# Softmax heads' first values by probabilities in three rounded products

## The reference

```python
def chunk_rel_attention(q, k, v, qn_g, kn_g, rel_bias):
    ...
    sc = jnp.where(valid[None, None, :, None, :], sc, NEG)
    p = jax.nn.softmax(sc, axis=-1)
    o = jnp.einsum('bhnqk,bnkhd->bhnqd', p, vb)
```

## Time and profile before

| | value |
|---|---|
| median of three executions | 1798.87 us (1797.88 to 1799.27) |
| the profiled execution: its own time | 1798.44 us |
| its span, first to last instruction | 1796.5 us |
| PE busy | 1786.8 us, 99% |
| DVE busy | 1246.1 us, 69% |
| ACT busy | 1052.9 us, 59% |
| POOL busy | 217.0 us, 12% |
| PE's granted clock, mean of the span | 0.999 of full speed |

### The profile page before, as it was taken

The page is one execution under the profiler, slowest core; times in us unless marked ns, Lnnn a source line. Parts: engine busy times, 40 slices in busy tenths (PEclk is TensorE's granted clock), DMA queues, the critical chain, the costliest instruction groups (busy, mean ns, idle before and its releaser), DMA issues.

```text
span 1796.5 us, 27448 instructions
## 1 busy us (share of the span) xinstructions
PE 1786.8 (99%) x10874; PEld 1621.4 (90%) x10874; DVE 1246.1 (69%) x1711; ACT 1052.9 (59%) x1702; POOL 217.0 (12%) x180
## 2 busy tenths in 40 slices
PE   9999999999999999999999999999999999999998
PEld 8999889888899999998889999898888999989987
DVE  6665656665666897687668888766565888767764
ACT  7436546774557765875554345686454445458853
POOL 0000000110011111100001322011000132311210
PEclk9999999999999999999999999999999999999999
DMA  9657555555655555454566655555565665555564
GB/s 367 199 175 223 186 182 190 178 177 192 193 185 173 167 173 169 155 172 164 190 209 201 202 190 177 194 177 175 188 191 197 200 199 186 174 191 182 172 220 140
DMA packets 95903, 340.32 MB, mean 189 GB/s; under 512 B 10800, under 2 KB 11184, under 8 KB 95648
## 3 DMA queue, kind: packets, MB, share of 16 engines
q1 hardware_dynamic: 94400, 334.44, 56.6%
q0 software_dynamic: 944, 3.61, 0.7%
q10 hardware_dynamic: 432, 0.53, 0.1%
HBM read 336.44 MB, written 2.10 MB: 188 GB/s over the span
## 4 chain that ended last, share of the span: by engine, by line
PE 99%; DMA 0%; DVE 0%; ACT 0%; issue 0%; DVEq 0%
PE ACC L848 15%; PE ACC L850 15%; PE ACC L849 15%; PE ACC L856 12%; PE ACC L853 12%; PE ACC L855 6%; PE ACC L854 6%; PE ACC L861 2%; PE ACC L862 2%; PE ACC L863 2%; PE PM L1015 1%; PE PM L993 1%; PE PM L900 1%; PE PM L970 0%; PE PM L1016 0%; PE PM L1063 0%
## 5 line engine op out<-in xcount | busy, mean ns | idle before, releaser
L1680 DVE TENSOR_TENSOR WL<-RAW,WH 128x1024 fp32r<-128x1024 f32 (+2 forms) x631 | 795.4, 1276 | 418.6 <-ACT WH L1239 417.2
L1239 ACT ACTIVATE WH<-RAW 128x1024 fp32r<-128x1024 f32 (+2 forms) x632 | 647.6, 1038 | 371.4 <-PE ACC L850 185.3
L856 PE MATMUL ACC<-XHL,WH 128*128 128x512 f32 x1024 | 391.2, 382 | 0.0
L853 PE MATMUL ACC<-XHL,WH 128*128 128x512 f32 x1024 | 390.3, 381 | 0.0
L848 PE MATMUL ACC<-WH,XHL 128*128 128x512 f32 (+1 forms) x788 | 295.9, 376 | 0.2 <-DVE WL L1680 0.2
L850 PE MATMUL ACC<-WH,XHL 128*128 128x512 f32 (+1 forms) x788 | 291.9, 370 | 0.0
L849 PE MATMUL ACC<-WL,XHL 128*128 128x512 f32 (+1 forms) x788 | 291.9, 370 | 0.0
L855 PE MATMUL ACC<-XHL,WL 128*128 128x256 f32 x1024 | 281.6, 275 | 0.0
L854 PE MATMUL ACC<-XHL,WL 128*128 128x256 f32 x1024 | 279.1, 273 | 0.0
L855 PEld LDWEIGHTS ACC<-XHL,WL 128*128 128x128 f32 x1024 | 193.5, 189 | 27.5
L854 PEld LDWEIGHTS ACC<-XHL,WL 128*128 128x128 f32 x1024 | 193.6, 189 | 25.9
(11 more groups left out here) (414 smaller groups left out, 2451.6 us busy)
## 6 DMA issues: line engine op xcount, KB each, us to landing
RAW<-in_w SPq DMA_DIRECT2D x607, 512.0 KB, 3.3
RAW<-in_wv SPq DMA_DIRECT2D x24, 344.0 KB, 3.2
X<-in_x SPq DMA_DIRECT2D x4, 512.0 KB, 12.1
Y<-in_xT SPq DMA_DIRECT2D x3, 512.0 KB, 10.7
out<-Y SPq DMA_DIRECT2D x6, 256.0 KB, 3.6
S<-in_bias POOLq DMA_DIRECT2D x8, 128.0 KB, 2.3
S<-in_od_gate_w POOLq DMA_DIRECT2D x1, 1024.0 KB, 7.3
S<-in_final_norm POOLq DMA_DIRECT2D x1, 1024.0 KB, 6.3
```

The lines of the kernel that those rows point to most:

```text
L853: e.matmul(acc[0], wh0, pairs, start=f, stop=False, skip_group_check=True)
L856: m = e.matmul(acc[1], wh1, pairs, start=False, stop=l, skip_group_check=True)
L1239: e.activation(hi, src, ACT.Copy).then_inc(s_hi)
L1680: e.tensor_tensor(lo, src, hi.bitcast(F32), ALU.subtract).then_inc(s_lo)
```

## The change

For the 32 heads with values 128 wide, the product of `v[0]` by the probabilities of all 256 tokens, one F32 product so far, becomes three rounded ones: high values by high probabilities, low by high, high by low. The product of `v[1]` stays in F32.

- `pT`, ACT: copies only the last 128 of the 384 columns as they are; the first 256 go rounded into `PH`, in a second instruction. It waits for the `pv` of the head before.
- `pl`, DVE, new: subtracts `PH` from PSUM into `PL`, 256 columns. It stands two slots after `pT`, in `after`; in the first eight heads of layer 3 half a slot after it, so in `before` of the next slot, ahead of the rope job's evacuation. The bank of PSUM is free for others only after it.
- `value_split`, new: three slots ahead of `pT`, ACT copies `v[0]` rounded (128 columns), and POOL subtracts (128 columns).
- `pv`, PE: waits for the low parts of the values and of the probabilities besides.
- The new buffer PVH takes the place of ZC, which is used in layer 1 alone. No bank and no transfer is added.

```diff
+        PH, PL = PVH[:, 0:256], PVH[:, 256:512]
...
                         put(slot + every * r + late, step, first + h + (4 if step[0] == "p" else 0), 1)
+                        if step == "pT":
+                            put(slot + every * r + late - 3, "value_split", first + h + 4)
+                            put(slot + every * r + (0.5 if first == 24 else 2) + late, "pl", first + h + 4)
...
-                read_out[b] = (s_pts, TURN[g])
+                read_out[b] = (s_pl, nth_narrow(g)) if narrow(g) else (s_pts, TURN[g])
...
                 if dv == 128:
-                    e.matmul(o[:, 0:256], v[0], p[:, 0:256], start=True, stop=False, skip_group_check=True)
+                    vh, vl = value_slot(g)
+                    e.wait_ge(s_vl, nth_narrow(g))
+                    e.wait_ge(s_pl, nth_narrow(g))
+                    e.matmul(o[:, 0:256], vh, PH, start=True, stop=False, skip_group_check=True)
+                    e.matmul(o[:, 0:256], vl, PH, start=False, stop=False, skip_group_check=True)
+                    e.matmul(o[:, 0:256], vh, PL, start=False, stop=False, skip_group_check=True)
                     e.matmul(o[:, 128:256], v[1], p[:, 256:384], start=False, stop=True, skip_group_check=True).then_inc(s_pv)
...
             def pT(g, b):
                 e.wait_ge(s_pt, TURN[g])
-                e.activation(pt_slot(g), PM[b][:, 0:384], ACT.Copy).then_inc(s_pts)
+                if not narrow(g):
+                    e.activation(pt_slot(g), PM[b][:, 0:384], ACT.Copy).then_inc(s_pts)
+                    return
+                if g > 4:
+                    e.wait_ge(s_pv, TURN[g] - 1)
+                e.activation(pt_slot(g)[:, 256:384], PM[b][:, 256:384], ACT.Copy).then_inc(s_pts)
+                e.activation(PH, PM[b][:, 0:256], ACT.Copy).then_inc(s_ph)
+
+            def value_split(g, _):
+                v, job = values_at(g)
+                n = nth_narrow(g)
+                e.wait_ge(s_evA, at_A(*job))
+                if n > 2:
+                    e.wait_ge(s_pv, TURN[g] - 2)
+                e.activation(value_slot(g)[0], v[0], ACT.Copy).then_inc(s_vh)
...
+            def probabilities_low(g, _):
+                b = PT_BANK[g]
+                e.wait_ge(s_ph, nth_narrow(g))
+                e.tensor_tensor(PL, PM[b][:, 0:256], PH.bitcast(F32), ALU.subtract).then_inc(s_pl)
...
+            def value_split(g, _):
+                v, _ = values_at(g)
+                vh, vl = value_slot(g)
+                e.wait_ge(s_vh, nth_narrow(g))
+                e.tensor_tensor(vl, v[0], vh.bitcast(F32), ALU.subtract).then_inc(s_vl)
```

More of the change, by code:

```diff
@@ L197, in program @@
         C = sb("C", CW)
-        ZC = sb("ZC", 1024)
+        with ExitStack() as first:
+            ZC = sb("ZC", 1024, F32, first)
+        PVH = sb("PVH", 1024, F32R)
         S5 = sb("S5", 2048)
@@ L278, in half_slot, with value_slot @@
             return [HALF[:, at + x:at + y] for x, y in ((0, 128), (128, 256), (256, 512), (512, 768))]
+        PH, PL = PVH[:, 0:256], PVH[:, 256:512]
+        def value_slot(g):
+            at = 512 + 256 * (g % 2)
+            return PVH[:, at:at + 128], PVH[:, at + 128:at + 256]
         def sc_slot(g):
@@ L416, in program, with values_at, narrow, nth_narrow @@
         TURN = list(accumulate(0 if g >= 4 and first_of_pair(g - 4) else 1 for g in range(44)))
+        def values_at(g):
+            layer, n, h = head_of(g - 4)
+            c = slice(128 * h, 128 * h + 128)
+            return [tok(3 * n + 2 if layer else 5)[:, t, c] for t in range(2)], (layer, f"v{n}" if layer else "va", h // 4)
+        def narrow(g):
+            return g >= 4 and not is_diff(g - 4)
+        def nth_narrow(g):
+            return g - 3 if g < 12 else g - 11
         def masked(a):
@@ L623, in program @@
                     FEW_BANK = got[0]
+        PT_BANK = {item: got for x in plan.values() for step, item, got in x if step == "pT"}
         def around(p):
@@ L657, in program @@
             sem(n) for n in ("s_dg", "s_pa", "s_pe", "s_pk", "s_pc", "s_pm", "s_zero", "s_am", "s_tri", "s_la"))
-        s_neg, s_hh, s_hl = sem("s_neg"), sem("s_hh"), sem("s_hl")
+        s_neg, s_hh, s_hl, s_ph, s_pl, s_vh, s_vl = (
+            sem(n) for n in ("s_neg", "s_hh", "s_hl", "s_ph", "s_pl", "s_vh", "s_vl"))
         s_lx, s_lc, s_ly, s_ld, s_so, s_sd, s_sa, s_or, s_on, s_gd1 = (
@@ L1004, in values_of @@
                     return [tok(2)[:, t, c] for t in range(2)], 256, (2, "v0", h // 4)
-                c = slice(128 * h, 128 * h + 128)
-                return [tok(3 * n + 2 if layer else 5)[:, t, c] for t in range(2)], 128, (layer, f"v{n}" if layer else "va", h // 4)
+                v, job = values_at(g)
+                return v, 128, job
             def pv(g, b):
@@ L1620, in scalar @@
             steps = {"seed": seed, "warm": warm, "xt": xt, "squares": squares, "root": root, "rms_a": rms_a, "gates1": gates1, "selectors": selectors, "decay_cols": decay_cols,
-                     "decay_rows": decay_rows, "cols": columns_step, "rows": rows, "decay": decay, "pT": pT,
+                     "decay_rows": decay_rows, "cols": columns_step, "rows": rows, "decay": decay, "pT": pT, "value_split": value_split,
                      "norm_qk": norm_qk, "qkT": qkT, "halves": halves, "scores": scores, "normal": normal, "silu_z": silu_z, "yT": yT, "mix1": mix1, "pv": pv, "ty": ty, "copied": copied, "silu": silu, "decays1": decays1,
@@ L2162, in vector @@
                      "decay": decay, "mscores": mscores, "norm_qk": norm_qk, "scale_k": scale_k, "scores": scores, "mix1": mix1,
-                     "mix2": mix2, "rsum": rsum, "pv": pv,
+                     "mix2": mix2, "rsum": rsum, "pl": probabilities_low, "pv": pv,
                      "yT": yT, "ty": ty, "taps": taps,
@@ L2320, in gained @@
                     e.tensor_tensor(Y3[:, t, c], X3[:, t, c], S0[:, c], ALU.mult).then_inc(s_gn)
-            steps = {"norm_qk": norm_qk, "scale_k": scale_k, "halves": halves, "scores": scores, "gate_z": gate_z, "cols": columns_step, "tri": tri, "gate_w": gate_w,
+            steps = {"norm_qk": norm_qk, "scale_k": scale_k, "halves": halves, "scores": scores, "value_split": value_split, "gate_z": gate_z, "cols": columns_step, "tri": tri, "gate_w": gate_w,
                      "gate_lru": gate_lru, "gate_c": gate_c, "load_mask": load_mask, "load_gain": load_gain, "gained": gained}
```

## The result

The changed kernel takes 1800.88 us (median of 22 executions, 1799.58 to 1803.43), against 1798.77 us before (median of 22, 1797.82 to 1800.30): 1.0013 times as long, 95% interval 1.0007 to 1.0019. That is 2.1 us slower where 2.3 was forecast: clear of the noise, but within the 0.2% that count as no change. The profiled execution took 1799.58 us, its span 1797.8.

What follows compares the result with a forecast made beforehand. PE, busy 99% of the span, sets the time. A 4.66 us delay in layer 3's first eight heads, less 0.24 given back and 2.1 saved, made 2.3 us slower: 1801.2 us on the median, range 1798.2 to 1804.2.

Steps and rivals of the forecast that it cites:

- PE's own part: Each changed head's pv group on PE falls from 0.65 to 0.57 us, 0.08 less; 2.6 us over 32 heads.
- The loop: ACT and DVE in layer 3's first eight heads: 0.07 plus 0.34, together 0.41 us more each round, on a 13.11 us period.
- Where it comes due: Layer 3's first eight heads: pv waits for the low part, reached at heads 32, 33, 34; PE 4.66 us later.
- None elsewhere: New pv waits on DVE's subtraction, about 3, 4 to 5 us in sum, only between 1545 and 1582 us.
- costed this rounding at nothing: ACT's rounding of `v[0]` falls where ACT waits 6.4 us for DVE; without that cover, 8 x 0.2 us.
- The sum: Whole kernel: 4.66 lost, less 0.24 given back and 2.1 saved by 26 heads, net 2.3 us slower.
- No stall: Rival: the loop gives way or the low part is ready earlier; 2.6 us faster, 3.2 at most; chance 0.13.
- POOL on DVE's port: Rival: POOL's added instruction gets ahead of DVE's waiting split, 0.4 us more a round; net 4.7 us slower; chance 0.18.
- No gain on PE: Rival: three rounded products cost what the F32 one did, stall as forecast; 4.4 us slower; chance 0.06.

Runs made afterwards that it cites:

- The extra subtraction: First eight heads of layer 3 back in F32, plus a DVE subtraction of 256 columns each round, result unused; 1799.12 us, ratio 1.0002 to the kernel before.
- The low part ahead of the split: Changed kernel, but in layer 3's first eight heads `pl` stands before DVE's next weight split; 1796.63 us, ratio 0.9987 to the kernel before.
- the low part early everywhere: Changed kernel, `pl` before the split in layer 3's first eight heads, ahead of the evacuation in all others; 1796.38 us, ratio 0.9989 to the kernel before.
- the low part behind the evacuation: Changed kernel, but in layer 3's first eight heads `pl` stands behind the rope evacuation of its slot; 1807.81 us, ratio 1.0045 to the kernel before.
- the stage alone: Change made only in layer 3's first eight heads, the other 24 keep the F32 product; 1804.74 us, ratio 1.0031 to the kernel before.

## Why the prediction was right, step by step

**PE's own part.** Right: 0.57 us for the group, from the scores' rows. Through layer 0 and layer 2 PE gains 0.61 us each over 8 heads, 0.076 a head, where 0.08 was taken.

**The loop.** Right: 13.50 us forecast and measured. DVE's part was 0.33 (0.34 taken), ACT's copies 0.42 (0.42 worked out, 0.07 in all taken for them). The extra subtraction shows that the added time isn't absorbed. The low part ahead of the split shows that it depends on the place: this the prediction did not see. It treated the loop as one that takes any addition in full.

**Where it comes due.** Right in place and size: 4.66 us forecast at head 34 and 4.66 measured from head 29 on (4.58 from head 28 on, from where the forecast counts), reached at heads 32, 33 and 34, the waits 4.5 us in sum. The savings of heads 28 to 33 are lost in it, and the 0.24 us of the earlier trace rows come back.

**"None elsewhere".** Wrong. Head 42 waits. The prediction costed the low part outside the first eight heads at nothing from head 41's margin, and reasoned that "the 0.4 us don't add up from round to round". From head 36 to head 40 that holds, in the two rounds behind them it does not. These are zT's evacuations of heads 40 and 42 on DVE and the pv of head 42 on PE, before, and then DVE after, at heads 40, 41 and 42:

```profile
1683.58 0.69 DVE L1705 TENSOR_TENSOR S<-S,ROWZ 128x512 f32<-128x512 f32 x1
...
1707.87 0.69 DVE L1705 TENSOR_TENSOR S<-S,ROWZ 128x512 f32<-128x512 f32 x1
...
1710.06 0.59 PE L1015 MATMUL PM<-SC,S 128*128 128x256 f32 x2
```

```profile
1684.86 0.69 DVE L1752 TENSOR_TENSOR S<-S,ROWZ 128x512 f32<-128x512 f32 x1
...
1697.87 0.69 DVE L1752 TENSOR_TENSOR S<-S,ROWZ 128x512 f32<-128x512 f32 x1
...
1710.26 0.69 DVE L1752 TENSOR_TENSOR S<-S,ROWZ 128x512 f32<-128x512 f32 x1
1710.87 0.42 DVE L1979 TENSOR_TENSOR PVH<-PM,PVH 128x256 fp32r<-128x256 f32 x1
```

DVE is 1684.86 - 1683.58 = 1.28 us later than before at head 40, 1697.87 - 1696.03 = 1.84 at head 41, and 1710.26 - 1707.87 = 2.39 at head 42: 0.56 and 0.55 us more in a round. PE is about 1 us later at all three (at head 42 1711.43 less its loss of 0.4, against 1710.06). Set against PE in this way, DVE is about 0.26 us late at each of heads 36 to 40 and no more from head to head, then 0.88 and 1.42. At head 42 the margin was 1.24 us: in the old times the low part would be ready at 1708.48 (where DVE's next instruction began) + 0.34 = 1708.82, and the pv began at 1710.06. So there the pv comes too early. It costs 0.4 us: 1711.43 against 1710.81 + 0.22 (the last product ahead of it, line 878, starts at 1710.81).

What grows are these two rounds of DVE themselves, 12.45 and 11.84 us before, 13.01 and 12.39 after. With the low part early everywhere they take 12.65 and 12.07. So 0.36 and 0.32 us of them come from the low part in its place, and go with it. The 0.2 us that stay may be ACT's, which copies in two instructions (0.05 us more) and rounds `v[0]` (0.19 us, from 1706.01 to 1706.20 in the trace after); the prediction costed this rounding at nothing, from the waits of ACT in the first eight heads. That is an estimate: no run took ACT's part away by itself.

**The sum.** PE's position against that of the trace before, from one stretch to the next, by the starts of the pv; the start-up (up to the first pv, head 4's) differs by -0.96 us between the two executions and is left out:

| stretch | forecast, us | measured, us |
|---|---|---|
| 16 heads of layers 0 and 2 | -1.28 | -1.22 |
| pause in layer 1, gone | not seen | -0.77 |
| first eight heads of layer 3 (4.66 - 0.24 - 2 x 0.08) | +4.26 | +4.26 |
| second eight of layer 3, head 42's wait in it, to the end | -0.64 | -0.01 |
| sum | +2.34 | +2.26 |

So the sum agrees in its main term, but its closeness owes something to luck: the pause gives 0.8 us, and head 42's wait takes about 0.5 (0.4 at its pv, and the saving of a head or two is lost in it). The prediction had neither. Nor had it the fall of the clock, 1.7 us in 9 of 22 executions, 0.7 on the mean, which the two traces behind this table don't have. At a mean clock of 0.999 alone the change costs 1800.32 - 1798.77 = 1.6 us by the medians, 0.7 less than by the two traces. Start-up is the likely place: in the eleven other traces head 4's pv begins between 0.96 us earlier and 1.94 us later than in the first, and 0.14 us later in the second trace of the same kernel. So of the 2.1 us measured some 0.6 are the clock's (1800.88 - 1800.32), and that it comes so close to 2.3 is chance.

**The rivals.** No stall: fell (waits of 4.5 us in the stage). POOL on DVE's port: fell in the changed kernel (3.43 us for the pair of splits, and nothing changes without POOL's subtraction); the rival's "more than twice its time" was read too high, since one by one the two splits of the earlier trace rows take 1.22 and 2.30 us; but in the kernel with the low part behind the evacuation the order of the two engines did turn over, for 0.15 us a round. No gain on PE: fell (0.57 against 0.65).

## What to carry to other kernels

Where a change saves on the engine that sets the time and puts the work on another, look for the one stage where the other has no lead left, and add up lateness there round by round: by the forecast 26 heads' savings of 2.1 us stood against one stage's 4.4. Inside such a loop the place of an added instruction counts for more than its length: put it into an idle gap that the loop already has (here the 1.1 us ahead of a split that waits for its partner), not behind the instruction that ends the gap. And don't take one head's margin for all: here DVE was 0.26 us late at each of five heads and 1.42 at the seventh, so every round's length is to be read, before and after.

## What had not been expected of the hardware

- After a wait of 2.0 us of PE the granted clock fell to 1.2 GHz for most of 3.4 us in one trace of the changed kernel and not in another, with the same wait at the same place; it cost 1.7 us. By their mean clock 9 of 22 executions had the fall. Behind the waits of 1.2 and 1.3 us at heads 32 and 33 in the same two traces the granted clock is 1.00, and so it is behind four waits of 1.45 us with the low part behind the evacuation.
- PE stood still for 0.6 us with no wait at one and the same instruction in both traces of the kernel before and both of the stage alone, and in none of the eight traces of kernels with the heads of layer 0 changed.
- Of DVE and POOL on their shared port, an instruction of 0.42 us between two others changed which engine came first, and with it who paid: 2.19 to 1.28 us for POOL's sum, 3.43 to 3.58 for DVE's pair of splits.
